# Recurrence keys of the second block mirrored into free columns, one product per level; meta values multiplied over 128 rows

## Chip, cores and metric

One core of one Trainium2 chip. The metric is device time in microseconds of one launch, the median of several executions; one further execution is profiled.

## What is computed

Two transformer blocks in float32 over 256 tokens, width 1024. The first block has differential attention with 16 meta tokens in front, a gated causal convolution of 31 taps and a feed-forward part. The second has attention over blocks (with 256 tokens, plain causal attention of 16 heads), a gated recurrence of 8 heads (hgrn2), attention to a memory of 256 tokens and a feed-forward part. Its recurrence, per head, with keys `k`, queries `q`, values `v` and log decays `g`:

```python
b = cumsum(gc)                                  # within a chunk
diff = b[t] - b[s]
decay = where(causal, exp(diff), 0)
a[t, s] = einsum('td,sd,tsd->ts', qc, kc, decay)
o = o_inter + a @ vc                            # o_inter: from the state before the chunk
```

The first block's attention is, per head, `(softmax(q1 k1) - lam * softmax(q2 k2)) @ v`, where the first 16 keys are the meta tokens.

## The kernel before

Everything is written out per engine (`@block.tensor`, `scalar`, `vector`, `gpsimd`, `sync`), with semaphores between them; each engine runs its list in that order, and no scheduler changes it. Activations lie with channels on the 128 partitions and tokens along the row.

**Weights.** They stream through a ring in 166 chunks of 128x2048 float32. A large product is made of three fast ones: weights and activations are each split into a high part (rounded to fp32r) and a low one, and high x high, high x low and low x high are added (`split_tile` and `split_by_token`, line 570: 24 matmuls a tile, two tiles a chunk). ScalarE rounds a chunk's high parts in two halves (`high_parts`, L1130) once a buffer of two is free; the low parts (`low_half`, L415, ring minus high part) are made one half on VectorE (`low_v`) and one on POOL (`low_g`). In heads1 POOL makes both. TensorE reads the low parts in the last third of a tile. Small products (scores, transposes, values, recurrence) are plain float32 matmuls, each of which is two records in the profile; the "x" counts of TensorE in the rows are records.

**heads1** (4 passes, two of the eight attention heads each, as four units `u`: head and half of the queries). The lists are `heads1` of each engine. Per unit TensorE makes scores (`scores1`, L697), transposes the combined probabilities (`turn1`, L704 for the 16 meta columns, L706) and multiplies the values (`values1`): L713 with the meta tokens' 16 rows (`v_meta[0:META]`, `a1M[0:META]`), then L715 with one or two blocks of 128 rows. VectorE writes maxima (`maxima1`), probabilities (`combine1`, L1711 and L1712) and, in between, the convolution taps (L1750) and its first two columns (`conv_lead`, L1730 to L1734).

**heads2** (4 passes, two recurrence heads and four attention heads each). The recurrence over 256 tokens is treated as two blocks of 128 and the cross part between them. Within a block the lower triangle is split into seven levels, `LEVELS` = 64, 32, ..., 1: on level m each stretch of 2m tokens gives keys from its first half and queries from its second, both scaled by exponentials of the distance to the middle. Per level x, POOL subtracts (L2431, L2432), ScalarE takes the exponential (`decay`, L1428), VectorE multiplies (`level`: keys into `kl`, L2026; queries into `ql`, L2028) and TensorE multiplies block by block (`level`, L930: 128 key columns, of which the unused half is zero, by 64 query columns, twice). `kl` is cleared once by POOL before the loop (L2414). Bank 7 first takes the diagonal (L940) and levels 0 and 1, bank 3 levels 2 to 5, bank 7 then level 6 and the cross product (L954): `hgrn_scores(h, 0..2)`. VectorE gathers them into `amat` (`gather0..2`: L2050 for the diagonal, L2042 a masked copy per level, with masks from the table, L2063). `hgrn_values` (L960, L962) multiplies with the values `iN`, the output of tiles 2 and 3.

Between them stand the attention's steps: rotation (`rotate`, L894; `rope_sin`, `rope_cos`, L2073 to L2078), scores (L903, L904), maxima (L2083 to L2086), exponentials (L1442, L1443), normalising (`normalise2`, L2090 to L2092, which frees `turn2`), transposes (L911), values (L923, L925). `cumulate` (L2009) scans the log decays of the next pass's heads; the fourth pass has none. ScalarE's list around the change is: copies of tiles 2 and 3, parts of chunk 3, `head_keys` (L1438), exponentials of levels 2 and 3, copies of tiles 4 and 5, parts of chunk 4, exponentials of levels 4 and 5, and so on. VectorE's list between the first rotation and the first transposes is: L2073, level 5, `gather0`, L2077 and L2078, level 6, cross products (L2033, L2034), low parts of chunk 5 (L415), `gather1`, second rotation, `gather2`, levels 7 and 8 (the second head's first two), scan, maxima, normalising. POOL's list is subtractions 0, 1, low 2, 2, 3, low 3, 4, 5, 6, low 4, 7, 8, low 5, 9, 10, low 6, 11, 12, 13, low 7 to 9; each subtraction waits until the exponential two before it is done.

## Time and profile before

| | |
|---|---|
| median of 3 runs | 1184.91 us (1183.97 to 1189.07) |
| profiled execution, its own time | 1187.4 us |
| its span, first to last instruction | 1185.8 us |
| mean granted TensorE clock | 0.985 of full speed |
| TensorE (PE) busy | 1141.6 us, 96% |
| VectorE (DVE) busy | 719.4 us, 61% |
| ScalarE (ACT) busy | 600.0 us, 51% |
| POOL (GpSimd) busy | 649.5 us, 55% |

heads1 lies from about 25 to 249 us of the span, down1 from 482 to 544, heads2 from 585 to 841. Busy time is that of instructions; a TensorE instruction's record is longer than its distance to the next, so the chain of waits, which counts from one to the next, gives its cost. PEld are the weight loads, which run beside the matmuls. Where an instruction is blocked after its start, its duration shows it.

### The profile page before, as it was taken

The page shows a single profiled execution, that of the slowest core. Times are in us where ns is not written, and L with a number is a line of the kernel's source. Part 1 is how long each engine was busy: PE and PEld are TensorE (multiplying, and loading weights), DVE is VectorE, ACT ScalarE, POOL GpSimd, SP SyncE. Part 2 cuts the span into 40 slices and gives each one's busy share as a digit, 9 for nine tenths or more (in the row PEclk, how much of TensorE's full clock was granted, in tenths as well). Part 3 has the DMA queues.
Part 4 walks back from the last instruction along what each step waited for, and adds up shares of the span by engine and source line. Part 5 has one row for each costly group of instructions (what it writes and reads, how often), then busy time and mean ns, then how long its engine had stood idle before and what let it go on. Part 6 is the DMA issues. An engine that isn't in the chain of part 4 may idle for free.

```text
span 1185.8 us, 24894 instructions
## 1 busy us (share of the span) xinstructions
PE 1141.6 (96%) x8962; PEld 1095.6 (92%) x8962; DVE 719.4 (61%) x1364; ACT 600.0 (51%) x1112; POOL 649.5 (55%) x451
## 2 busy tenths in 40 slices
PE   6999999999889999999899999999999999999997
PEld 6999999998779999999899989898999989999996
DVE  5675766688656777525875856757666546444322
ACT  5644444455255656437555455555535455444332
POOL 4666666660355666644763637364375436656542
PEclk9999999999889999998999999999999999999998
DMA  8444444341343454543433423333445425545531
GB/s 324 145 147 141 156 141 161 142 147 72 142 178 114 173 192 169 205 148 137 164 126 109 162 99 122 141 109 139 147 174 172 149 90 195 178 177 198 193 143 36
DMA packets 26209, 179.43 MB, mean 151 GB/s; under 512 B 2848, under 2 KB 4128, under 8 KB 4768
## 3 DMA queue, kind: packets, MB, share of 16 engines
q1 hardware_dynamic: 25856, 178.28, 42.2%
q8 instruction: 43, 0.70, 0.2%
q10 hardware_dynamic: 288, 0.27, 0.1%
q14 instruction: 22, 0.18, 0.0%
HBM read 177.49 MB, written 1.05 MB: 151 GB/s over the span
## 4 chain that ended last, share of the span: by engine, by line
PE 77%; DVE 11%; issue 6%; POOL 2%; ACT 2%; DVEq 0%; DMA 0%; POOLq 0%; ACTq 0%
PE ps L570 51%; PE ps L852 10%; PE ps L930 2%; POOL parts L415 2%; PE ps L636 1%; PE ps L485 1%; DVE ps L2185 1%; DVE act L1823 1%; PE ps L667 1%; PE ps L610 1%; DVE branch L1964 1%; PE ps L923 1%; ACT parts L1130 1%; DVE parts L415 1%; PE ps L533 1%
## 5 line engine op out<-in xcount | busy, mean ns | idle before, releaser
L415 POOL TENSOR_TENSOR parts<-ring,parts 128x1024 fp32r<-128x1024 f32 x208 | 513.5, 2479 | 478.2 <-ACT parts L1130 475.1
L570 PE MATMUL ps<-x_high,parts 128*128 128x256 f32 (+2 forms) x3088 | 417.4, 284 | 4.3 <-DVE glu L1999 2.2
L570 PEld LDWEIGHTS ps<-x_high,parts 128*128 128x128 f32 x3088 | 387.2, 189 | 15.1 <-issue 8.1
L1130 ACT ACTIVATE parts<-ring 128x1024 fp32r<-128x1024 f32 x324 | 323.9, 1049 | 138.5 <-PE ps L852 69.3
L415 DVE TENSOR_TENSOR parts<-ring,parts 128x1024 fp32r<-128x1024 f32 x116 | 151.8, 1309 | 127.3 <-ACT parts L1130 127.3
L570 PE MATMUL ps<-x_low,parts 128*128 128x256 f32 (+2 forms) x1520 | 214.5, 284 | 0.0
L570 PEld LDWEIGHTS ps<-x_low,parts 128*128 128x128 f32 x1520 | 196.3, 189 | 0.0
L1750 DVE SCALAR_TENSOR_TENSOR ps<-glu,table_sb,ps 128x256 f32<-128x256 f32 x232 | 93.3, 479 | 0.6 <-DVE ps L1750 0.2
L852 PE MATMUL ps<-act_high,parts 128*128 128x256 f32 x704 | 87.8, 280 | 0.0
L852 PEld LDWEIGHTS ps<-act_high,parts 128*128 128x128 f32 x704 | 85.1, 188 | 0.0
L570 PE MATMUL ps<-parts,x_high 128*128 128x256 f32 x448 | 62.3, 285 | 0.9 <-DVE work L2098 0.9
L570 PEld LDWEIGHTS ps<-parts,x_high 128*128 128x128 f32 x448 | 56.4, 188 | 3.0 <-issue 3.0
L1109 ACT ACTIVATE work<-ps 128x256 f32<-128x256 f32 (+2 forms) x52 | 19.9, 385 | 74.9 <-PE ps L570 72.1
L852 PE MATMUL ps<-act_low,parts 128*128 128x256 f32 x352 | 46.5, 282 | 0.0
L852 PEld LDWEIGHTS ps<-act_low,parts 128*128 128x128 f32 x352 | 43.8, 189 | 0.0
L1100 ACT ACTIVATE work<-work 128x256 f32<-128x256 f32 x44 | 18.3, 418 | 49.0 <-DVE work L2275 33.0
L1100 ACT ACTIVATE work<-ps,table_sb 128x256 f32<-128x256 f32 x44 | 24.5, 558 | 33.7 <-PE ps L570 29.7
L1964 DVE TENSOR_TENSOR branch<-work 128x256 f32 (+1 forms) x22 | 34.4, 1561 | 3.8 <-DVE work L1959 2.3
L2431 POOL TENSOR_TENSOR sq<-conv 128x128 f32 x56 | 25.4, 454 | 19.7 <-ACT sq L1428 16.1
L1100 ACT ACTIVATE sq<-res 128x256 f32<-128x256 f32 (+2 forms) x48 | 18.2, 412 | 34.3 <-DVE res L1873 27.0
L485 PE MATMUL ps<-conv,ring 128*128 128x258 f32 x128 | 31.6, 410 | 3.6 <-DVE x_high L1836 3.6
L485 PEld LDWEIGHTS ps<-conv,ring 128*128 128x128 f32 x128 | 25.6, 205 | 9.3 <-issue 3.9
(331 smaller groups left out, 1611.0 us busy)
## 6 DMA issues: line engine op xcount, KB each, us to landing
ring<-weights SPq DMA_DIRECT2D x166, 1024.0 KB, 4.8
res<-h_in SPq DMA_DIRECT2D x4, 272.0 KB, 3.7
act<-mem SPq DMA_DIRECT2D x1, 1024.0 KB, 14.9
out<-xT SPq DMA_DIRECT2D x4, 256.0 KB, 2.5
table_sb<-table SPq DMA_DIRECT2D x1, 969.5 KB, 9.0
table_sb<-table ACTq DMA_DIRECT2D x1, 132.5 KB, 3.5
work<-positions ACTq DMA_DIRECT2D x1, 128.0 KB, 4.7
```

The lines of the kernel that those rows point to most:

```text
L415: eng.tensor_tensor(parts[:, LOW - HIGH + p, cols], ring[:, slot, cols], parts[:, p, cols].bitcast(F32), ALU.subtract)\
L485: mm = pe.matmul(ps[:, b, 0:width], ring[:, slot, k * CW + e * P:k * CW + e * P + P], moving(k), start=k == 0, stop=k == KB - 1)
L533: mm = pe.matmul(ps[:, 4, c * wide:(c + 1) * wide], sq[:, k, s:s + P], weight(k), start=k == 0 and c == 0, stop=k == KB - 1, skip_group_ch ...
L570: mm = pe.matmul(out, left(k), right(k), start=step_ == 0 and k == 0, stop=step_ == 2 and k == KB - 1)
L852: mm = pe.matmul(ps[:, DOWN_BANK + t // 2, t % 2 * SEQ:(t % 2 + 1) * SEQ], w[:, kk * D + t * P:kk * D + t * P + P], x[:, kb + kk, 0:SEQ], ...
L930: mm = pe.matmul(ps[:, bank, at + HD * blk:at + HD * blk + HD], kl[:, l, blk * P:blk * P + P], ql[:, l, blk * HD:blk * HD + HD], start=Tru ...
L1100: ins = sc.activation(out, src, fn, **kw)
L1109: sc.activation(out, src, fn, scale=scale).then_inc(tile_read[b], 1)
L1130: sc.activation(parts[:, p, cols], ring[:, slot, cols], ACT.Copy).then_inc(split_high, 1)
L1750: ve.scalar_tensor_tensor(acc, u, w, acc, ALU.mult, ALU.add).then_inc(dve_step, 1)
L1964: ve.tensor_tensor(branch[:, j + (e - 2), 0:SEQ], silu_g[:, 2 * (g % 2) + e - 2, :], acc, ALU.mult)\
L2431: gp.tensor_tensor(d[:, :, 0, :], middle, b[:, :, 0, :], ALU.subtract)
```

## The change

1. Mirrored keys. `kl` has 128 columns a level instead of 256. The first block's keys stay in the first halves of each stretch; the second block's are written backwards, so that they fall on the second halves, which were zero. VectorE writes them with a second product, `ql` as before. TensorE makes one product per level, 128 key columns by 128 query columns (both blocks). The keys of a column's other block come out as scores too, and the masks leave them out.
2. What follows from it. The second block's scores have their rows in mirrored order, so its keys for the diagonal (`head_keys`, now four copies of 128 columns) are mirrored, the diagonal is taken with `both_diagonals` (identity and mirrored identity), and the second block's values are mirrored once per pass: `mirror_values`, one product 128x256 on TensorE after tile 4, through bank 2, which ScalarE copies back to `iN[:, 1]`. The masks and `both_diagonals` are made on VectorE during down1 (`mirrored_constants`). The clearing of `kl` on POOL is gone.
3. Meta values. `v_meta` and `a1M` are cleared once by POOL at the start (ScalarE waits for it in the first pass), and `values1` multiplies all 128 rows, where rows 16 to 127 are zero.

```diff
         ones, ident = col("ones", 0, P), col("ident", 0, P)
+        masks = col("level_masks", 0, len(LEVELS) * P).bitcast(I32).rearrange("p (l c) -> p l c", c=P)
...
         kh = carve(gluf, 0, HEADS, SEQ)
+        both_diagonals = carve(gluf, HEADS * SEQ, 2 * P)
         attf = branch[:, :, :].rearrange("p a b -> p (a b)")[:, 2 * KB * TQ:3 * KB * TQ]
...
         kh_s = carve(actf, 4480, 2, SEQ)
-        kl = carve(resf, 0, len(LEVELS), SEQ)
+        kl = carve(resf, 0, len(LEVELS), P)
         cross_e = carve(resf, 1792, 2, P)
...
         meta_shift, meta_exp, meta_probs, meta_T, meta_done = (sem(n) for n in ("meta_shift", "meta_exp", "meta_probs", "meta_T", "meta_done"))
-        att_gated = sem("att_gated")
+        values_mirrored = sem("values_mirrored")
+        att_gated, meta_cleared = sem("att_gated"), sem("meta_cleared")
         centered, conv_root, conv_scaled, conv_act = (sem(n) for n in ("centered", "conv_root", "conv_scaled", "conv_act"))
...
                 hold(pe, bank_read[7], n.before(bank_read[7]))
-                pe.matmul(ps[:, 7, 0:P], v_meta[0:META, h * P:h * P + P], a1M[0:META, :], start=True, stop=False)
+                pe.matmul(ps[:, 7, 0:P], v_meta[:, h * P:h * P + P], a1M, start=True, stop=False)
                 for j in range(u % 2 + 1):
...
+            def mirror_values(i):
+
+                b = STREAM.bank("heads2", 3)
+                hold(pe, bank_read[2], n.before(bank_read[2]))
+                pe.wait_ge(tile_read[b], STREAM.before("heads2", i, 3) + 1)
+                pe.matmul(ps[:, 2, 0:CW], both_diagonals[:, P:2 * P], iN[:, 1, :], start=True, stop=True)\
+                  .then_inc(values_mirrored, 1)
+
             def scores2(j):
...
             def level(h, l, bank, at):
-                for blk in range(2):
-                    mm = pe.matmul(ps[:, bank, at + HD * blk:at + HD * blk + HD], kl[:, l, blk * P:blk * P + P],
-                                   ql[:, l, blk * HD:blk * HD + HD], start=True, stop=True)
-                return mm
+                return pe.matmul(ps[:, bank, at:at + P], kl[:, l, :], ql[:, l, :], start=True, stop=True)
...
-                for t in range(6):
+                for t in range(5):
                     proj(t)
+                mirror_values(i)
+                proj(5)
                 hgrn_scores(0, 0)
...
                 if start:
+                    sc.wait_ge(meta_cleared, 2)
                     root_of_mean(7, SEQ, D, "eps6", root[:, 0:SEQ], rooted)
...
             def head_keys(i, h):
-                sc.activation(kh_s[:, h, :], kh[:, i * 2 + h, :], ACT.Copy).then_inc(khs_ready, 1)
+                sc.activation(kh_s[:, h, 0:P], kh[:, i * 2 + h, 0:P], ACT.Copy)
+                sc.activation(kh_s[:, h, SEQ - 1:P - 1:-1], kh[:, i * 2 + h, P:SEQ], ACT.Copy).then_inc(khs_ready, 1)
...
                 head_keys(i, 1)
+                sc.wait_ge(values_mirrored, n.next(values_mirrored))
+                sc.activation(iN[:, 1, :], ps[:, 2, 0:CW], ACT.Copy).then_inc(bank_read[2], 1)
                 decay(2)
...
-            down_low("down1")
+            def mirrored_constants():
+
+                ve.tensor_copy(both_diagonals[:, 0:P], ident)
+                ve.tensor_copy(both_diagonals[:, P:2 * P], ident[:, ::-1])
+                at = 0
+                for l, m in enumerate(LEVELS):
+                    blocks = ident
+                    if m > 1:
+                        blocks = conv_f[:, at:at + P // m]
+                        step(ve.tensor_reduce(blocks, ident.rearrange("p (j i) -> p j i", i=m), AX, ALU.add))
+                        at += P // m
+                    ve.tensor_copy(masks.bitcast(F32)[:, l, P // 2:P].rearrange("p (b i) -> p b i", i=m),
+                                   blocks[:, ::-2].rearrange("p (b o) -> p b o", o=1).to_broadcast([P, P // (2 * m), m]))
+
+            down_low("down1", mirrored_constants)
             low_v("forget", 0, 0)
...
-            masks = col("level_masks", 0, len(LEVELS) * P).bitcast(I32).rearrange("p (l c) -> p l c", c=P)
-
             def halves(x, m):
...
                 ve.wait_ge(decay_ready, n.next(decay_ready))
-                e = halves(el[:, x % 2, :], m)
-                ve.tensor_tensor(halves(kl[:, l, :], m)[:, :, 0, :], halves(kh[:, i * 2 + h, :], m)[:, :, 0, :],
-                                 e[:, :, 0, :], ALU.mult)
+                e, keys = halves(el[:, x % 2, :], m), halves(kh[:, i * 2 + h, :], m)
+                b = P // (2 * m)
+                ve.tensor_tensor(halves(kl[:, l, :], m)[:, :, 0, :], keys[:, 0:b, 0, :], e[:, 0:b, 0, :], ALU.mult)
+                ve.tensor_tensor(halves(kl[:, l, :], m)[:, ::-1, 1, ::-1], keys[:, b:, 0, :], e[:, b:, 0, :], ALU.mult)
                 ve.tensor_tensor(ql[:, l, :].rearrange("p (b m) -> p b m", m=m), halves(qh[:, h, :], m)[:, :, 1, :],
...
                 ve.wait_ge(bank_full[7], n.next(bank_full[7]))
-                step(ve.tensor_tensor(amat[:, 0:2, :], ps[:, 7, 0:SEQ].rearrange("p (a b) -> p a b", b=P),
-                                      ident.rearrange("p (o b) -> p o b", o=1).to_broadcast([P, 2, P]), ALU.mult))
+                step(ve.tensor_tensor(diag, ps[:, 7, 0:SEQ], both_diagonals, ALU.mult))
                 place(0, 7, 256, dve_step)
...
+            gp.memset(v_meta, 0.0).then_inc(meta_cleared, 1)
+            gp.memset(a1M, 0.0).then_inc(meta_cleared, 1)
             gp.memset(rinv[:, 0:TQ], 0.0).then_inc(pool_step, 1)
...
                 low_g("heads2", 0, c)
-            gp.wait_ge(cum_ready, 2)
-            gp.memset(kl, 0.0).then_inc(pool_step, 1)
-            gp.wait_ge(pool_step, n.next(pool_step))
             with gp.Fori(0, 4) as i:
```

How the instructions stand, first on TensorE around the copy of tile 5 in heads2 (names: `x_high`, `x_low_55` and `parts` are activations and weight parts, `sq` is `ql`, `res` is `kl`). Before, tiles 4 and 5, the diagonal of head 0 and its levels 0 and 1:

```order
L581 ISA
L570 MATMUL ps<-x_high,parts 128x256 x8
L570 MATMUL ps<-x_low_55,parts 128x256 x8
L570 MATMUL ps<-x_high,parts 128x256 x8
L221 REGISTER_ALU
L570 MATMUL ps<-x_high,parts 128x256 x8
L570 MATMUL ps<-x_low_55,parts 128x256 x8
L570 MATMUL ps<-x_high,parts 128x256 x8
L221 ISA
L937 ISA
L938 ISA
L940 MATMUL ps<-work,act 128x128 x2
L930 MATMUL ps<-sq,res 128x64 x4
```

The same place after the change:

```order
L573 MATMUL ps<-x_high,parts 128x256 x8
L221 ISA
L904 REGISTER_ALU
L905 MATMUL ps<-work,glu 128x256
L573 MATMUL ps<-x_high,parts 128x256 x8
L573 MATMUL ps<-x_low_55,parts 128x256 x8
L573 MATMUL ps<-x_high,parts 128x256 x8
L221 REGISTER_ALU
L945 ISA
L946 ISA
L948 MATMUL ps<-work,act 128x128 x2
L940 MATMUL ps<-sq,res 128x128 x2
```

The mirroring product (L905) stands between tiles 4 and 5, and two wide level products take the place of four narrow ones.

On VectorE, heads2, the end of the first rotation's product, level 6, the cross products and the low parts of chunk 5. Before:

```order
L2078 TENSOR_TENSOR work<-work 128x512
L2024 REGISTER_ALU
L2026 TENSOR_TENSOR res<-glu,sq 128x128
L2028 TENSOR_TENSOR sq<-work,sq 128x128
L2032 REGISTER_ALU
L2033 TENSOR_TENSOR sq<-glu,res 128x128
L2034 TENSOR_TENSOR res<-work,res 128x128
L414 ISA
L415 TENSOR_TENSOR parts<-ring,parts 128x1024
```

After:

```order
L2104 TENSOR_TENSOR work<-work 128x512
L2050 REGISTER_ALU
L2053 TENSOR_TENSOR res<-glu,sq 128x64
L2054 TENSOR_TENSOR res<-glu,sq 128x64
L2055 TENSOR_TENSOR sq<-work,sq 128x128
L2059 REGISTER_ALU
L2060 TENSOR_TENSOR sq<-glu,res 128x128
L2061 TENSOR_TENSOR res<-work,res 128x128
L417 ISA
L418 TENSOR_TENSOR parts<-ring,parts 128x1024
```

One product more per level, in two of 64 columns; the order around it is the same.

On ScalarE, heads2, between the parts of chunk 3 and the exponential of level 2. Before:

```order
L1130 ACTIVATE parts<-ring 128x1024 x2
L1438 ISA
L1438 ACTIVATE act<-glu 128x256
L1438 ISA
L1438 ACTIVATE act<-glu 128x256
L1426 REGISTER_ALU
L221 REGISTER_ALU
L1428 ACTIVATE sq<-sq 128x256
```

After:

```order
L1140 ACTIVATE parts<-ring 128x1024 x2
L1449 ISA
L1449 ACTIVATE act<-glu 128x128
L1450 ISA
L1450 ACTIVATE act<-glu 128x128
L1449 ISA
L1449 ACTIVATE act<-glu 128x128
L1450 ISA
L1450 ACTIVATE act<-glu 128x128
L1501 REGISTER_ALU
L1502 ACTIVATE work<-ps 128x256
L1437 REGISTER_ALU
```

Four half copies for two whole ones, and the copy of the mirrored values with its wait (L1501) ahead of the exponential.

## Rows read from the trace of the kernel before

**Rows 1.** The page, part 1: busy us, share of the span, instructions.

```profile
PE 1141.6 (96%) x8962; PEld 1095.6 (92%) x8962; DVE 719.4 (61%) x1364; ACT 600.0 (51%) x1112; POOL 649.5 (55%) x451
```

**Rows 2.** Stretches of heads2's third pass: start:end, length, PE, PEld, DVE, ACT, POOL busy, clock, DMA.

```profile
661.90:727.30 65.40, 65.40 (x511) 60.62 (x510) 43.43 (x100) 34.97 (x77) 32.88 (x37) 1.00 0.36 128
667.20:683.60 16.40, 16.40 (x131) 15.41 (x130) 14.12 (x37) 6.65 (x15) 8.57 (x10) 1.00 0.52 192
```

**Rows 3.** The chain that ended last, third pass of heads2: start us, us, what.

```profile
662.17 0.44 PE ps L940 x4
...
667.21 2.83 PE ps L570 x24
670.04 1.73 PE ps L930 x16
...
683.59 0.33 PE ps L911 x3
...
702.67 0.48 PE ps L911 x3
...
705.99 0.43 PE ps L960 x2
```

**Rows 4.** VectorE in order of time, third pass: start us, us, what [idle before].

```profile
653.59 2.27 DVE L2026 TENSOR_TENSOR res<-glu,sq 128x128 f32<-128x128 f32 x1 [0.15 <-ACT sq L1428]
...
667.25 0.69 DVE L2073 TENSOR_TENSOR work<-ps,work 128x512 f32<-128x512 f32 x1 [1.72 <-PE ps L894]
667.86 0.42 DVE L2026 TENSOR_TENSOR res<-glu,sq 128x128 f32<-128x128 f32 x1
668.20 0.48 DVE L2028 TENSOR_TENSOR sq<-work,sq 128x128 f32<-128x128 f32 x1
...
672.19 1.21 DVE L415 TENSOR_TENSOR parts<-ring,parts 128x1024 fp32r<-128x1024 f32 x1
...
678.83 1.36 DVE L2009 TENSOR_TENSOR_SCAN conv<-table_sb,conv 128x128 f32 x4
...
682.55 0.35 DVE L2092 TENSOR_SCALAR work<-work,small 128x256 f32<-128x256 f32 x1
...
697.80 1.73 DVE L415 TENSOR_TENSOR parts<-ring,parts 128x1024 fp32r<-128x1024 f32 x1
...
701.91 0.35 DVE L2092 TENSOR_SCALAR work<-work,small 128x256 f32<-128x256 f32 x1
```

**Rows 5.** Groups of VectorE: a product of 64 and one of 128 columns.

```profile
L1680 DVE TENSOR_TENSOR table_sb<-table_sb x1: 214/214/214, 19.6 to 19.6; 128x64 f32<-128x64 f32 x1
...
L2034 DVE TENSOR_TENSOR res<-work,res 128x128 f32<-128x128 f32 x8 | 2.2, 280 | 0.0
```

**Rows 6.** POOL in order of time, third pass of heads2.

```profile
653.21 2.50 POOL L415 TENSOR_TENSOR parts<-ring,parts 128x1024 fp32r<-128x1024 f32 x1 [1.75 <-ACT parts L1130]
...
664.97 0.40 POOL L2431 TENSOR_TENSOR sq<-conv 128x128 f32 x1 [1.91 <-ACT sq L1428]
...
665.75 2.37 POOL L415 TENSOR_TENSOR parts<-ring,parts 128x1024 fp32r<-128x1024 f32 x1
...
672.43 3.23 POOL L415 TENSOR_TENSOR parts<-ring,parts 128x1024 fp32r<-128x1024 f32 x1 [1.52 <-ACT parts L1130]
...
696.09 2.35 POOL L415 TENSOR_TENSOR parts<-ring,parts 128x1024 fp32r<-128x1024 f32 x1 [5.06 <-ACT parts L1130]
```

**Rows 7.** The chain that ended last, third pass of heads1, around two values1 calls.

```profile
183.25 0.41 PE ps L713 x2
183.66 0.42 PE ps L715 x2
...
187.66 0.64 PE ps L715 x4
```

**Rows 8.** TensorE in order of time, third pass of heads1, the third transposes.

```profile
176.20 0.28 PE L704 MATMUL ps<-table_sb,work 128*16 128x128 f32 x1 [0.24 <-DVE work L1712]
```

**Rows 9.** VectorE in order of time, a chunk of down1.

```profile
494.55 1.23 DVE L415 TENSOR_TENSOR parts<-ring,parts 128x1024 fp32r<-128x1024 f32 x1 [4.45 <-ACT parts L1130]
```

More of the change, by code:

```diff
@@ L164 @@
 BODY[('tensor', 'heads1')] = {'kv_ready': 1, 'bank_read4': 4, 'probs_ready': 4, 'bank_read6': 4, 'bank_read7': 4}
-BODY[('tensor', 'heads2')] = {'roped': 2, 'bank_read7': 4, 'khs_ready': 2, 'level_ready': 16, 'bank_read2': 3, 'bank_read3': 4, 'bank_read4': 4, 'probs_ready': 4, 'bank_read5': 4, 'bank_read6': 1}
+BODY[('tensor', 'heads2')] = {'roped': 2, 'bank_read7': 4, 'khs_ready': 2, 'level_ready': 16, 'bank_read2': 4, 'bank_read3': 4, 'bank_read4': 4, 'probs_ready': 4, 'bank_read5': 4, 'bank_read6': 1}
 BODY[('scalar', 'heads1')] = {'bank_full4': 4, 'max_ready': 4, 'probs_ready': 4, 'bank_full6': 4, 'bank_full7': 4}
@@ L168 @@
 BODY[('scalar', 'up2')] = {'gate_act': 4}
-BODY[('scalar', 'heads2')] = {'bank_full7': 4, 'diff_ready': 14, 'level_ready': 16, 'bank_full4': 4, 'max_ready': 8, 'bank_full3': 4, 'bank_full5': 4, 'bank_full8': 4}
+BODY[('scalar', 'heads2')] = {'values_mirrored': 1, 'bank_full7': 4, 'diff_ready': 14, 'level_ready': 16, 'bank_full4': 4, 'max_ready': 8, 'bank_full3': 4, 'bank_full5': 4, 'bank_full8': 4}
 BODY[('vector', 'heads1')] = {'bank_full4': 4, 'dve_step': 79, 'bank_read4': 4, 'bank_full6': 4, 'conv_ready': 2}
```

## Prediction

> **What bounds the kernel now.** I read the page first, then the busy time by stretches, then the chain of waits, and at last the instructions in order of time on all four engines through one pass of the heads2 loop (the third, 661.9 to 727.3 us; the other passes repeat it 65.4 us apart). TensorE is busy 96% of the span and through the whole of that pass, which moved nothing but its own work [rows 1, 2]. Read alone, that says: shorten TensorE and the time falls. The next view limits this. I cut a pass at the instructions where TensorE takes something from VectorE: **A**, from the end of the first rotation (L894, 667.21) to the first softmax's transposes (L911, 683.59); **B**, from there to the fourth softmax's transposes (702.67); **C**, the rest. In A VectorE is busy 14.1 of 16.4 us, and what is left are waits for its own last instruction [rows 2]. It starts at 667.25, when the rotation is there, and has the probabilities at 682.55 + 0.35 = 682.90; TensorE takes them at 683.59, some 0.5 later than a handing over needs [rows 3, 4]. In B its chain of normalising, four levels, maxima, weight parts and normalising ends at 701.91 + 0.35 = 702.26, and TensorE takes the result at 702.67: some 0.25 to spare [rows 3, 4]. So A and B are almost as long on VectorE as on TensorE. C has TensorE alone.
>
> **The level products.** Each was two products over 64 columns, now one over 128. Eight old products take 1.73 (each stands as two records), 0.216 a product [rows 3]; two 128-column products of the same type take 0.44, 0.22 a product [rows 3]. A level falls from 0.43 to 0.22. Per pass that is 2 levels in C (0.43), 4 + 1 in A (1.08), 2 + 4 in B (1.30) and the last in B (0.22): 3.0, in four passes 12.1. The added mirroring product (128x256, as L960) costs 0.43 in C [rows 3]. C comes out even, and all depends on what A and B do with their 2.6.
>
> **A.** VectorE gets one product more per level. A 64-column product takes 0.214, a 128-column one 0.280 [rows 5], so splitting one costs two times 64 columns and a second start: 0.07 at least. The upper end is a product beside POOL's subtractions, 0.48 against 0.28, some 0.41 to the next start [rows 4]. A holds levels 5 to 8. TensorE would come to the transposes 1.08 earlier, VectorE gets there 0.3 later at best, and 0.5 lay between: with nothing else, TensorE waits 0.9 and A ends as before. But there is a race. VectorE starts half of chunk 5's weight parts (L415) at 672.19, POOL its half at 672.43, and POOL then takes 3.23 instead of 2.45: it waited. Where POOL is first, VectorE waits: the key product at 653.59 took 2.27, ending when POOL's did, and the weight parts at 697.80 ended 1.09 after POOL's [rows 4, 6]. By these rows the loser of the race pays a whole POOL instruction. The Trainium skill ("SBUF — State Buffer", Who interferes with whom) has this as a rule: a VectorE instruction with two SBUF inputs and a GpSimd one that reads SBUF exclude each other, and the first to start keeps the port for its whole length. By that rule, the trace agrees.
>
> Who is first after the change? The margin is 672.43 - 672.19 = 0.24 [rows 4, 6], and 0.23 to 0.25 in all four passes. The mirroring product stands before tile 5, so tile 5 ends 0.43 later. ScalarE's parts of chunk 4 and the exponential behind them follow it, POOL's subtraction at 664.97 waits for that exponential, and POOL's L415 at 665.75 comes behind it [rows 6]: it now ends at 668.55, not 668.12. The level-5 key product at 667.86 already had to wait for that end [rows 4], so it is 0.43 later, and the added products of levels 5 and 6 give 0.14 more: VectorE comes to its L415 at 672.75 or later. POOL's start hangs on ScalarE's parts of chunk 5, hence on tile 7, which isn't later: the 0.43 before tile 5 is given back by the two levels behind it. POOL is first. VectorE's parts end at 672.43 + 2.45 + 1.09 = 675.97, not 673.40: +2.57, and what follows them is dense. Less 0.1 for POOL work that no longer meets the rotation's products, plus 0.14 for levels 7 and 8: the probabilities come 2.6 later, at 685.5, and TensorE takes them at 685.6 instead of 683.59. **A: +2.0.** I take 0.07 for each added product here, since the row nearest to them, 128 columns in 0.280, ran beside nothing; at 0.41 each, A would end at +2.7, and with VectorE first in the race near 0.
>
> **B.** The second softmax's scores and their maxima move by 2.1. Then come levels 9 to 12 with an added product each, 4 x 0.07 = 0.3 to 4 x 0.41 = 1.6; in the third pass POOL's small subtractions meet only two or three of those products, so 0.4. The weight parts behind them stay second to POOL's, as they are now [rows 6]. The 0.3 that lay before the last transposes hides part: 2.1 + 0.4 - 0.25. **A and B together: +2.25 a pass**, and TensorE's 2.6 goes into three waits. The fourth pass has no scan of the next heads (four instructions, 1.36 [rows 4]) before the first maxima: there the scores and not VectorE come last, +0.9 after A, +1.05 after B. heads2: 3 x 2.25 + 1.05 = **+7.8**.
>
> **The meta values.** values1 multiplies 16 rows before products of 128 rows. In the chain L713 takes 0.41 and the first L715 behind it 0.42, while the next L715, again 128 rows after 128 rows, adds 0.64 - 0.42 = 0.22 [rows 7]. So each change of rows costs 0.19 to 0.20, and a call has two: 0.39. With 128 rows both go. There are 16 calls. In passes 2 to 4 of heads1 the first two stand before the third transposes, where TensorE already waits for VectorE [rows 8]: those six calls give nothing. Ten give 0.39: **-3.9**. The Trainium skill ("TensorE: Matmul & The Clock Gate", Why this matters for your kernels) says that a lone product over 32 rows takes the same time as over 128. By it this part is worth 0; the rows say 0.39 a call, since they also hold the hand-over between sizes. I take the rows. Behind heads1 the convolution's VectorE chain starts from TensorE's meta scores, so the gain goes on to the end.
>
> **At nothing:** the constants on VectorE in down1 (about 15 small instructions, some 4 us) lie in an idle time of 4.45 per chunk [rows 9], and the parts behind them are wanted only when the next chunk's low products begin; without that cover they would cost their 4 us once. The two memsets on POOL come before its first work. The removed memset lies beside tiles. On ScalarE two more key copies and the mirrored copy (0.35 each at most) delay the decays of levels 2 and 3 by 1.0, and VectorE can't use those before POOL's parts end anyway; if it could, POOL's work of 664.97 would still be what is late.
>
> **Sum.** -3.9 + 7.8 + 0 = +3.9. The profiled execution (span 1185.8, time 1187.4) would show about 1191.3; the median of the runs, 1184.9, becomes **1188.8**. About 0.5%, 5.9 us, is what a measurement of this kernel can tell from no change.
>
> **Rivals.**
> 1. *VectorE stays first in the race.* For it: every added product may hide in waits that I count as dense. Against: 0.14 + 0.43 is twice the margin. A then ends +0.2, B +0.1 more, heads2 +1.2: **1182.2**. 0.17.
> 2. *TensorE's own time decides*, as the 96% suggest. For it: no wait for VectorE of over 0.2 is seen in heads2. Against: the ends at 682.90 and 702.26. Full price -12.1 + 1.7 - 6.2: **1168.3**; with room in A alone (4 x 1.08) 1177, in B alone (4 x 1.52) 1175. 0.20.
> 3. *The slower side: each added product waits out a POOL subtraction*, 0.41 instead of 0.07 to 0.1. It decides once POOL's subtractions stand beside levels 9 to 12 in each pass: 4 x 0.34 x 4 = 5.4 more, **1194.2**. 0.08.
> 4. *The widened meta product gains nothing*, by the small-row equality worked into this kernel: +3.9, **1192.7**. 0.05. (That is the TensorE page's rule.)
> The forecast has 0.50, of which 0.12 lies above 1190.8. That the products don't get shorter is no rival of its own: TensorE has time to spare in A and B, and C would lose 1.7.
>
> **Range and chances.** 1176 to 1195 holds the forecast, rivals 1, 3 and 4 and the upper third of rival 2; somewhat under 2 in 10 is left out, nearly all below. Faster by over 0.5%: 0.20 (rival 2). Slower by over 0.5%: 0.12 + 0.08 + 0.05 = 0.25. Within: 0.55.
>
> **What will show it.** Level products half as many and 0.22 each. In each heads2 pass VectorE's weight parts before the copies of levels 2 to 5 last some 3 us instead of 1.2, POOL's 2.45 instead of 3.23, and TensorE waits 1 to 2 us before the first scores (L903 now) and again before the transposes (L911 now). A pass of 67.6 instead of 65.4. Heads1 3.9 shorter, L713's successor at 0.22. I am wrong if POOL's parts still take 3.2, if the passes fall under 65, or if heads1 is as long as before.

## The result, and the profile after

| | before | after |
|---|---|---|
| median of the runs | 1185.57 us (11 runs, 1183.97 to 1189.07) | 1191.41 us (11 runs, ten of them 1190.13 to 1193.77) |
| ratio after to before | | 1.0049, 95% interval 1.0036 to 1.0061 |
| span of the profiled execution | 1185.8 us | 1188.9 us |
| mean granted TensorE clock | 0.985 | 0.989 |

One run of the changed kernel took 3531.9 us and has no part in the ratio. The change costs 5.8 us; the interval leaves out 1, and the cost lies just under the 5.9 us that the prediction took as the least that can be told from no change. Page of the changed kernel, part 1; it answers to [rows 1]:

```profile
PE 1123.9 (95%) x8858; PEld 1079.8 (91%) x8858; DVE 743.8 (63%) x1435; ACT 601.2 (51%) x1124; POOL 645.9 (54%) x452
```

TensorE is busy 17.7 us less and the kernel is slower: what it saved became waiting. The place is found by laying the starts of ScalarE's 324 weight parts (L1130 before, L1140 after) side by side. The difference is -1.3 us at the end of heads1's first pass, -3.6 at the end of heads1, -6.3 from 360 us to 530, -6.8 as heads2 begins, then +2.9 a pass in three passes and +1.5 in the fourth, and +3.2 from there to the end. So heads1 gave 3.6, heads2 cost 10.2, and nothing behind heads2 moved.

The step from -3.6 to -6.8 is not the change. Stretches of the kernel before (start:end, length, busy time of PE, PEld, DVE, ACT, POOL, then clock and DMA):

```profile
250.00:270.00 20.00, 19.71 (x153) 18.70 (x153) 16.77 (x46) 11.63 (x24) 14.21 (x6) 0.91 0.48 171
...
345.00:480.00 135.00, 131.00 (x1058) 129.73 (x1058) 99.92 (x143) 82.85 (x127) 81.23 (x62) 0.97 0.49 170
545.00:585.00 40.00, 35.70 (x275) 35.05 (x274) 29.80 (x53) 26.88 (x48) 22.39 (x15) 0.91 0.41 148
```

The same stretches of the changed kernel:

```profile
250.00:270.00 20.00, 18.80 (x152) 17.86 (x150) 18.04 (x48) 12.33 (x31) 11.21 (x5) 1.00 0.45 159
...
345.00:480.00 135.00, 133.95 (x1094) 132.91 (x1095) 102.77 (x145) 84.03 (x127) 81.59 (x63) 0.99 0.48 168
545.00:585.00 40.00, 36.70 (x296) 35.65 (x296) 33.99 (x55) 25.80 (x42) 26.74 (x22) 0.99 0.40 142
```

The profiled execution of before had more time at TensorE's lower level of 1.2 GHz (0.91 against 1.00 in the first stretch). This is not the change: e4, e6 and e9 below make the changed kernel's instructions there and their profiles show 0.91 in the first stretch, while e5, e7, e8 and e13 show 1.00. So it is luck of one execution, and it is why the spans differ by 3.1 us and the medians by 5.8: the profiled execution of before lies 1.8 over its median, that of the changed kernel 0.9 under its own. The instructions' own sum, 10.2 - 3.6 = 6.6, fits the medians.

Heads1, the chain that ended last, first pass (start us, us, what), after the change:

```profile
51.94 0.22 PE ps L716 x2
52.16 0.22 PE ps L718 x2
...
59.16 0.22 PE ps L716 x2
59.38 0.45 PE ps L718 x4
```

L716 was L713: 0.41 has become 0.22, and its successor's first product is 0.22, where it was 0.42 [rows 7].

Heads2's third pass. VectorE in order of time (start us, us, what, idle before), from the rotation on, with the first L2053 to L2055 for level 5, the second for level 6, and L2060, L2061 for the cross part:

```profile
663.26 0.69 DVE L2099 TENSOR_TENSOR work<-ps,work 128x512 f32<-128x512 f32 x1 [1.21 <-PE ps L897]
663.87 0.88 DVE L2053 TENSOR_TENSOR res<-glu,sq 128x64 f32<-128x64 f32 x1
664.67 0.44 DVE L2054 TENSOR_TENSOR res<-glu,sq 128x64 f32<-128x64 f32 x1
...
668.23 0.21 DVE L2053 TENSOR_TENSOR res<-glu,sq 128x64 f32<-128x64 f32 x1
668.37 0.21 DVE L2054 TENSOR_TENSOR res<-glu,sq 128x64 f32<-128x64 f32 x1
668.50 0.28 DVE L2055 TENSOR_TENSOR sq<-work,sq 128x128 f32<-128x128 f32 x1
668.70 2.48 DVE L2060 TENSOR_TENSOR sq<-glu,res 128x128 f32<-128x128 f32 x1
671.10 0.48 DVE L2061 TENSOR_TENSOR res<-work,res 128x128 f32<-128x128 f32 x1
671.51 1.43 DVE L418 TENSOR_TENSOR parts<-ring,parts 128x1024 fp32r<-128x1024 f32 x1
...
682.06 0.35 DVE L2118 TENSOR_SCALAR work<-work,small 128x256 f32<-128x256 f32 x1
```

POOL beside it, low parts of chunks 4 and 5:

```profile
662.27 2.39 POOL L418 TENSOR_TENSOR parts<-ring,parts 128x1024 fp32r<-128x1024 f32 x1
...
668.53 2.51 POOL L418 TENSOR_TENSOR parts<-ring,parts 128x1024 fp32r<-128x1024 f32 x1 [0.77 <-ACT parts L1140]
```

And every wait of TensorE in that pass:

```profile
671.64 0.49 PE L940 MATMUL ps<-sq,res 128*128 128x128 f32 x2 [1.01 <-DVE res L2061]
676.90 0.48 PE L914 MATMUL ps<-work 64*128 64x128 f32 x2 [1.71 <-DVE work L2104]
682.46 0.55 PE L922 MATMUL ps<-table_sb,work 128*128 128x128 f32 x3 [0.96 <-DVE work L2118]
701.51 0.55 PE L922 MATMUL ps<-table_sb,work 128*128 128x128 f32 x3 [1.25 <-DVE work L2118]
```

The port (that for which VectorE and POOL exclude each other) went to POOL, as forecast, but one step earlier: it is the cross product L2060 that lasts 2.48 instead of 0.28, and the low parts L418 come after it with 1.43. TensorE, which waited for nothing here before, now waits 4.9 us a pass, 3.7 of them in A. By the prediction's cuts (chain of waits) A grew from 16.38 to 682.46 - 663.23 = 19.23, B went from 19.08 to 19.05, and C stayed at 29.9 to 30.0. All of the +2.86 a pass is A.

### The profile page after: what moved, and what is told of

It reads as the page before. It is cut to its first block, busy times and chain, and to the rows that moved or that the text cites. A ratio compares the mean times of both kernels' runs of the same rounds, so it can differ in the third digit from the quotient of the medians.

```text
span 1188.9 us, 24789 instructions
## 1 busy us (share of the span) xinstructions
PE 1123.9 (95%) x8858; PEld 1079.8 (91%) x8858; DVE 743.8 (63%) x1435; ACT 601.2 (51%) x1124; POOL 645.9 (54%) x452
## 3 DMA queue, kind: packets, MB, share of 16 engines
HBM read 177.49 MB, written 1.05 MB: 150 GB/s over the span
## 4 chain that ended last, share of the span: by engine, by line
PE 62%; DVE 18%; issue 9%; POOL 5%; ACT 4%; DVEq 1%; DMA 0%; ACTq 0%; POOLq 0%
PE ps L573 43%; PE ps L855 10%; POOL parts L418 3%; DVE parts L418 2%; PE ps L639 1%; ACT parts L1140 1%; DVE ps L2211 1%; DVE act L1837 1%; PE ps L488 1%; DVE act L2069 1%; DVE branch L1978 1%; DVE sq L2060 1%; POOL sq L2341 1%; PE ps L613 1%; POOL res L2436 1%
## 5 line engine op out<-in xcount | busy, mean ns | idle before, releaser
L418 POOL TENSOR_TENSOR parts<-ring,parts 128x1024 fp32r<-128x1024 f32 x208 | 512.8, 2476 | 480.8 <-ACT parts L1140 477.9
L1140 ACT ACTIVATE parts<-ring 128x1024 fp32r<-128x1024 f32 x324 | 323.9, 1049 | 138.5 <-PE ps L855 69.3
L418 DVE TENSOR_TENSOR parts<-ring,parts 128x1024 fp32r<-128x1024 f32 x116 | 156.2, 1347 | 120.8 <-ACT parts L1140 120.7
```

Of the source, the lines that this page charges most:

```text
L418: eng.tensor_tensor(parts[:, LOW - HIGH + p, cols], ring[:, slot, cols], parts[:, p, cols].bitcast(F32), ALU.subtract)\
L1140: sc.activation(parts[:, p, cols], ring[:, slot, cols], ACT.Copy).then_inc(split_high, 1)
```

## The experiments

For all kernels I measured each pass by records of TensorE: **A** from the start of the first rotation to the start of the first transposes, **B** from there to the fourth transposes, **C** to the next pass's first rotation. For the kernel before:

```profile
666.19 1.02 PE L894 MATMUL ps<-work,table_sb 128*128 128x512 f32 x2
...
683.42 0.49 PE L911 MATMUL ps<-table_sb,work 128*128 128x128 f32 x3
...
702.60 0.55 PE L911 MATMUL ps<-table_sb,work 128*128 128x128 f32 x3
```

A is 17.23 (it holds the rotation, and so is longer than the prediction's), B 19.18. By records A grows by 3.03 with the change and B falls by 0.13, where the chain of waits has +2.85 and -0.03: where TensorE doesn't wait, the record of the first transposes starts 0.17 before its place in the chain (683.42 for 683.59) and that of the fourth 0.07. The pass is the same by both. Passes shown are ones with the clock at 1.00. Others have a stretch at 1.2 GHz and are longer: e5 67.3 and 67.2, e6 67.3, e7 68.6 twice, e13 69.7 and 68.2. Each ratio is to the kernel before on the same chip.

| kernel | ratio (95%) | median us | A | B | C | pass |
|---|---|---|---|---|---|---|
| before | 1 | 1184.4 to 1185.8 | 17.23 | 19.18 | 28.95 | 65.36 |
| changed | 1.0049 (1.0036 to 1.0061) | 1191.4 | 20.26 | 19.05 | 28.92 | 68.23 |
| e1 meta part alone | 0.9965 (0.9952 to 0.9979) | 1181.7 | 17.23 | 19.18 | 28.95 | 65.36 |
| e2 keys alone | 1.0104 (1.0086 to 1.0122) | 1197.6 | 20.24 | 19.07 | 28.92 | 68.23 |
| e5 exponential before both halves | 1.0021 (1.0009 to 1.0034) | 1188.1 | 18.92 | 19.07 | 28.93 | 66.91 |
| e8 exponential between halves | 0.9990 (0.9975 to 1.0004) | 1184.2 | 17.87 | 19.06 | 28.93 | 65.86 |
| e6 low parts of chunk 7 first | 1.0017 (1.0003 to 1.0031) | 1187.1 | 20.26 | 17.73 | 28.93 | 66.92 |
| e7 scan late | 1.0052 (1.0034 to 1.0069) | 1191.8 | 19.15 | 19.02 | 28.93 | 67.10 |
| e9 = e8 + e6 + e7 | **0.9904** (0.9885 to 0.9924) | **1174.6** | 16.76 | 17.69 | 28.93 | 63.38 |
| e10 old keys, e6 + e7, meta | 0.9962 (0.9949 to 0.9975) | 1180.9 | 17.23 | 19.18 | 28.95 | 65.36 |
| e4 mirroring product later | 1.0053 (1.0037 to 1.0068) | 1191.4 | 20.09 | 19.06 | 28.95 | 68.10 |
| e11 split keys on the kernel before | 1.0021 (1.0005 to 1.0038) | 1188.6 | 17.38 | 19.24 | 28.95 | 65.57 |
| e12 the product alone on before | 1.0020 (1.0007 to 1.0034) | 1187.9 | 17.23 | 19.18 | 29.37 | 65.77 |
| e13 levels 0 and 1 made twice | 1.0060 (1.0047 to 1.0073) | 1192.5 | 19.38 | 19.07 | 29.37 | 67.81 |

**The two parts apart.** e1 is the kernel before with

```diff
-pe.matmul(ps[:, 7, 0:P], v_meta[0:META, h * P:h * P + P], a1M[0:META, :], start=True, stop=False)
+pe.matmul(ps[:, 7, 0:P], v_meta[:, h * P:h * P + P], a1M, start=True, stop=False)
```

and the clearing; e2 is the changed kernel without these lines.

> The kernel before with only the meta change (all 128 rows of v_meta and a1M, cleared at the start). If the two parts of the change are independent, heads1 is 3.6 us shorter, as in the profile of the change, and nothing else moves: 1182.0 us against 1185.6. If the gain needed the rest of the change, or came from something else, less than 1 us. If every one of the 16 calls gave its 0.39, 6.2 us: 1179.4.

> The change without its meta part (16 rows again). If the loss lies in the heads2 passes alone (68.25 us a pass for 65.39 in three, 1.5 more in the fourth), it is 10.1 us slower than before: 1195.7, and heads1 as long as before. If the constants made in down1 or the clearing at the start cost something of their own, more than 1198.

e1: 4.1 us faster, heads1 3.6 shorter in its trace, heads2 as before to 0.01. e2: 11.8 by the medians, 12.3 by the ratio; its passes are those of the changed kernel, heads1 is as long as before. Its total is 2 us above the expectation; in its profile heads2 costs 10.1, as expected, so the rest is between executions. By the ratios the two parts come to +0.7% and the whole change to +0.5%, which the intervals allow. By the passes the parts are independent, and the whole loss is in the mirrored keys.

**Is it the port, and nothing else, in A?** e5 holds POOL's parts of chunk 5 back, e8 does it without making VectorE wait:

```diff
 e5
-                ahead2(3)
                 decay(7)
+                ahead2(3)
 e8
-                ahead2(3)
-                decay(7)
+                ahead2(3, lambda: decay(7))
...
                 for half in (1, 0):
                     sc.activation(parts[:, p, cols], ring[:, slot, cols], ACT.Copy).then_inc(split_high, 1)
+                    if half and between:
+                        between()
```

> The changed kernel with ScalarE's exponential of level 7 ahead of its parts of chunk 5. POOL's low parts of chunk 5 then wait until about 7 us after the end of the first rotation instead of 5.3, and VectorE's cross products and low parts (5.5 and 5.9 us after it) come first. Race theory: the cross product takes 0.28 instead of 2.48, VectorE's low parts 1.25, and POOL's run beside the masked copies and the rotation's product from PSUM, which they do not block. VectorE's chain to the first probabilities is 2.5 us shorter; TensorE waits 0.4 there, a pass is 65.9 to 66.2 us, the total about 1183. Rival, that the added products and their collisions are the cost and the race is only where they show: pass over 67.4, total over 1188.

> The changed kernel with ScalarE's exponential of level 7 between the two halves of its parts of chunk 5. In the run with the exponential ahead of both halves VectorE won the port but stood idle 1.03 us for its half. Now VectorE's half is ready when it comes to it, about 5.9 us after the end of the first rotation, and POOL's is ready at about 6.0: VectorE is first by 0.1. If it is, cross products 0.28 each, low parts 1.25 with no idle time before, A 1.0 shorter than in that run (about 17.9 from the start of the first rotation to the transposes, for 20.26 in the changed kernel) and a pass of 65.9; total about 1183.5. If POOL is first by a little, the low parts take 3.5 and the pass 68.

e8's VectorE and then POOL, third pass (L2061, L2062 are the cross products):

```profile
669.74 0.28 DVE L2061 TENSOR_TENSOR sq<-glu,res 128x128 f32<-128x128 f32 x1
669.94 0.28 DVE L2062 TENSOR_TENSOR res<-work,res 128x128 f32<-128x128 f32 x1
670.14 1.21 DVE L418 TENSOR_TENSOR parts<-ring,parts 128x1024 fp32r<-128x1024 f32 x1
...
671.29 2.40 POOL L418 TENSOR_TENSOR parts<-ring,parts 128x1024 fp32r<-128x1024 f32 x1 [2.50 <-ACT parts L1140]
```

Cross product 0.28, low parts 1.21, and POOL right behind them, beside work that it doesn't block. A fell by 2.39, to the 17.9 and the pass of 65.9 that were expected, and the total by 7 us to that of the kernel before. In e5 the cross product was free too, but the exponential waited for POOL's subtraction, ScalarE's parts came late, and VectorE stood 1.03 us idle for them: A 18.92 and not 17.9. That is a miss of 1 us a pass (expected: a pass of 65.9 to 66.2), and e8 was made from it. So losing the port costs 2.4 of the 2.9 us a pass. The other 0.5 stays in e8. There VectorE still comes to the cross product 6.49 after the rotation's start, for 5.59 before; that the 0.5 is what is left of this lateness (the added products and the wait at level 5) is argued, and no run takes it away alone.

**Is B's wait the port as well?** 

```diff
-                low_values(i, 0)
                 low_v("heads2", i, 7)
+                low_values(i, 0)
```

> The changed kernel with VectorE's low parts of chunk 7 ahead of the low parts of the first attention values. VectorE idles 1.7 us there until ScalarE has rounded those values, and its half of chunk 7 is ready at the start of that idle time. It then has the port before POOL: 1.23 us instead of 2.52, inside the idle time. The last maxima of the pass start when the scores are there, 2.4 us earlier, TensorE waits nothing before the fourth transposes (1.25 now), and stretch B is TensorE's own: 17.8 us for 19.05. Pass 67.0 instead of 68.2, total about 1186.5. Rival, that in B something else than this chain is late too: B over 18.6, total over 1189.5. A as it is (the port is lost at the cross product as now).

e6's VectorE and then POOL in B:

```profile
695.66 1.23 DVE L418 TENSOR_TENSOR parts<-ring,parts 128x1024 fp32r<-128x1024 f32 x1
697.25 0.42 DVE L2129 TENSOR_TENSOR ya_low<-ps,ya_high 128x256 f32 x1 [0.37 <-ACT ya_high L1466]
...
696.65 2.47 POOL L418 TENSOR_TENSOR parts<-ring,parts 128x1024 fp32r<-128x1024 f32 x1 [5.13 <-ACT parts L1140]
```

2.52 has become 1.23, POOL's 2.38 is 2.47, B is 17.73: TensorE's own time, as expected.

**Is VectorE's chain all there is in A?** e7 moves the scan into idle time of C:

```diff
-                if scan:
-                    ve.wait_ge(log_ready, 2)
-                    cumulate(i + 1)
                 maxima2(0)
...
                 low_values(i, 1)
+                if scan:
+                    ve.wait_ge(log_ready, 2)
+                    cumulate(i + 1)
```

> The changed kernel with the scan of the next heads (four instructions, 1.36 us in all) moved from ahead of the first maxima to behind the second low parts of attention values, where VectorE idles 2.5 us and 5 us before POOL reads it. If VectorE's chain alone sets A in passes 1 to 3, A is 1.28 shorter there and as it was in the fourth: pass 66.95, three times 1.28, total about 1187.5. If the scan is hidden in A (TensorE's scores late as well), under 0.5 a pass, total over 1190.

In the first pass A is 19.15, 1.1 shorter: right. In the second and third it is 20.69, and the total hasn't moved. The same 10 us of A in its three passes:

```profile
609.00:619.00 10.00, 8.29 (x62) 7.36 (x61) 8.13 (x23) 3.41 (x9) 1.26 (x3) 1.00 0.55 211
676.00:686.00 10.00, 8.29 (x52) 7.58 (x51) 8.12 (x23) 3.33 (x8) 1.24 (x3) 0.83 0.56 210
744.00:754.00 10.00, 8.29 (x51) 7.43 (x52) 8.13 (x23) 3.24 (x9) 1.37 (x3) 0.83 0.56 210
```

Equal busy time, but at 0.83 part of the stretch ran at 1.2 GHz, behind the wait of 1.71 for the scores; it costs 1.54 a pass, more than the scan gave. The seven executions show a mean clock of 0.982 to 0.987, those of the kernel before 0.987 in the mean. So the mechanism was right, and in this profile the lower clock took back what it gave; for the other executions only their mean clock says so. e5, e6 and e13 have such a stretch too, e2 and e4, with as much waiting in a pass, have none in heads2.

**Together, and with the old keys.** e9 is the changed kernel with e8's, e6's and e7's edits. e10 is e1 with e6's and e7's (VectorE has the port there already).

> All three together on the changed kernel: exponential of level 7 between the halves, VectorE's low parts of chunk 7 first, the scan late. If the three causes are all that keeps TensorE waiting in heads2, its own time is left: A 16.2 us (17.23 before, 20.26 in the changed kernel, from the start of the first rotation), B 17.9, C 28.9, a pass of 63.0 for 65.4 before, some 2 us less in the fourth, and with the meta part 13 us under the kernel before: 1173. If a next wait comes up (ScalarE's exponentials or the second rotation), passes of 64 to 65 and 1176 to 1179.

> The kernel before with the meta part, VectorE's low parts of chunk 7 first and the scan late, but with the old keys and the two narrow products a level. There TensorE never waits in heads2, so room on VectorE buys nothing: A 17.23, B 19.18, C 28.95, a pass of 65.4 as before, and the same time as the meta part alone, 0.9965 of the kernel before. Against it the run with all three and the mirrored keys (0.9904) shows what the mirrored keys are worth once VectorE has room: 2 us a pass. If these moves were good by themselves, this run would be under 0.994.

e9 is the fastest kernel of the case: 1174.6 us, 1.0% under the kernel before. Its heads2 has one wait of TensorE left from the first rotation to the fourth transposes:

```profile
672.95 0.48 PE L914 MATMUL ps<-work 64*128 64x128 f32 x2 [0.58 <-DVE work L2105]
```

It is 1.6 us over the expectation: A is 16.76, not 16.2, since VectorE still reaches the scores 0.58 late. e10 has the passes of the kernel before and the time of e1. So the two moves are worth nothing where TensorE sets the pass, and the mirrored keys, a loss of 10 us as they were put in (1.0049 against e1's 0.9965), gain 6 to 7 once VectorE has room (0.9904 against 0.9962). e10 leaves out e8's edit, so that this holds for the old keys with the two moves that they can use.

**What made VectorE late?** e4 moves the mirroring product:

```diff
-                mirror_values(i)
                 proj(5)
                 hgrn_scores(0, 0)
+                mirror_values(i)
```

and ScalarE's copy of it behind `ahead2(2)`. e11 is the kernel before with the key product split in two (`for part in (slice(0, b), slice(b, 2 * b))`, each 64 columns). e12 is the kernel before with a product after tile 4, by the identity, and its copy.

> The changed kernel with the mirroring product after tile 5 and the scores (not after tile 4), and ScalarE's copy of it after the parts of chunk 4. The 0.43 us still lie before the rotation, but no longer between tile 5 and POOL's low parts of chunk 4. Race theory: POOL's low parts of chunk 4 end 0.43 earlier against the rotation, so the keys of level 5 are not blocked (0.44 or less instead of 0.88), VectorE is at the cross product before POOL starts its low parts of chunk 5 and gets the two cross products through (0.2 to 0.5 each), but loses the port for its own low parts of chunk 5, which take 3.3 to 3.7. Pass 67.8 us, total about 1189.5. Rival, that the 0.43 before the rotation and the added products set the pass and the port only shows it: pass unchanged at 68.2.

> The kernel before with VectorE's key product of each level split in two of 64 columns, and nothing else changed: one part of the change alone, with TensorE's work as before. If the added products are enough to lose the port (0.34 at level 5, beside POOL's subtractions, and 0.07 at level 6, against a margin of 0.24), VectorE's low parts of chunk 5 or a cross product take 2.4 to 3.6 us, POOL's low parts there 2.4 to 2.5 instead of 3.23, A is 2.3 to 2.6 longer, a pass 67.7 to 68.1 and the total about 1194. If it takes the mirroring product's 0.43 as well, POOL's parts still take 3.1 or more, A is 0 to 0.3 longer and the total within 2 us of the kernel before.

> The kernel before with the product after tile 4 and ScalarE's copy alone (with the identity, so that the values stay as they are). TensorE has 0.43 more work a pass, VectorE none. If the prediction's step holds, that this product puts POOL's low parts of chunk 4 and with them the level-5 keys 0.43 later and so flips the race alone, A is 2.1 to 2.5 longer and a pass 67.9. If POOL's parts of chunk 4 are held by something that is not later (ScalarE's exponentials before them), VectorE stays first and a pass is 65.8 us: total 1.7 over the kernel before.

All three missed. e4 brought 0.13 a pass, close to its rival's pass of 68.2: the copy now stands before the exponentials that POOL's list waits for, so POOL's parts of chunk 4 were hardly earlier, and VectorE came to the cross product at 6.33 (from the rotation's start), POOL to its parts of chunk 5 at 6.26. e12 flipped nothing and cost its 0.41 in C: the product puts tile 5, the rotation and VectorE later alike. In the changed kernel the rotation comes earlier again against tile 5, by the two narrowed levels between them; that half was missing. e11 made VectorE 0.45 later at the cross product (0.36 for the added product at level 5, beside POOL's subtractions, not 0.07; the rest at level 6), and yet kept the port: POOL's parts 3.70, A +0.15. So neither part alone turned the race. e13 joins them: in the changed kernel levels 0 and 1 of the first head are made twice, so that the rotation stands as late against tile 5 as before.

```diff
+                    if h == 0:
+                        level(h, 0, 7, 256)
+                        level(h, 1, 7, 384)
                     level(h, 0, 7, 256)
                     level(h, 1, 7, 384).then_inc(bank_full[7], 1)
```

> The changed kernel with the first head's products of levels 0 and 1 made twice, between tile 5 and the tile before the first rotation: 0.43 us of pure waste on TensorE a pass, in the place of the 0.43 that the change took out there. If it is the earlier rotation against tile 5 (and so against POOL's low parts of chunk 4) that adds the last 0.46 of VectorE's lateness, the rotation is 0.43 later against POOL, the keys of level 5 are blocked 0.5 and not 0.88, VectorE comes to the cross product about 6.0 after the start of the rotation, as in the run with the split keys alone, and keeps the port: cross products 0.3, low parts 1.25, POOL's 3.7. A about 17.4 for 20.26, B 19.0, C 28.9 + 0.43, a pass of 65.8 for 68.2 and a total some 8 us under the changed kernel, about 1183. If the port is lost all the same, the passes are 68.2 to 68.7 and the total 1191 to 1193.

e13's VectorE and then POOL; the first row is level 5's keys, 0.42 as before the change:

```profile
666.08 0.42 DVE L2056 TENSOR_TENSOR res<-glu,sq 128x64 f32<-128x64 f32 x1
...
670.65 0.28 DVE L2064 TENSOR_TENSOR res<-work,res 128x128 f32<-128x128 f32 x1
670.85 3.41 DVE L418 TENSOR_TENSOR parts<-ring,parts 128x1024 fp32r<-128x1024 f32 x1
...
664.04 2.37 POOL L418 TENSOR_TENSOR parts<-ring,parts 128x1024 fp32r<-128x1024 f32 x1
...
670.66 2.53 POOL L418 TENSOR_TENSOR parts<-ring,parts 128x1024 fp32r<-128x1024 f32 x1 [1.15 <-ACT parts L1143]
```

e11's, which should be the same race:

```profile
672.75 0.32 DVE L2036 TENSOR_TENSOR res<-work,res 128x128 f32<-128x128 f32 x1
672.96 1.25 DVE L415 TENSOR_TENSOR parts<-ring,parts 128x1024 fp32r<-128x1024 f32 x1
...
672.76 3.70 POOL L415 TENSOR_TENSOR parts<-ring,parts 128x1024 fp32r<-128x1024 f32 x1 [1.15 <-ACT parts L1130]
```

The lateness is now accounted for: from the rotation's start VectorE reaches the cross product at 5.59 before, 6.04 with the added products (e11, e13 alike), and 6.50 with level 5's keys blocked 0.46 longer as well. The outcome of the race at 6.04 isn't: POOL starts at 6.24 and VectorE's low parts at 6.44 in both, in each of four passes, and e11's VectorE got the port, e13's POOL (low parts 3.41). So the lateness alone doesn't settle who is first, and why the port was lost in the changed kernel is shown only as far as its lateness goes. One thing differs between the two: e11's products just before last 0.30 to 0.32, e13's 0.28. So e13's expected gain of 8 us did not come; A fell by 0.9 in its first pass (the second and third hold a stretch at the lower clock, and the total is no better), by the blocked time at level 5 and the cross products that slipped through.

## Why the prediction was right or wrong

Predicted 1188.8 with 1176 to 1195, and 0.55 for less than 0.5% either way; measured 1191.4, 5.8 us over the kernel before. That it came out within 0.5% is luck: the forecast was a cost of 3.9, and against the 1184.9 that the prediction started from, 1191.4 is 6.5 more; only against the 1185.57 of 11 runs is it 5.8, just under the line of 5.9. By its steps:

- **What bounds the kernel, and the races: right.** TensorE had 96% and lost 18 us of work for nothing; the end was set by the hand-overs that the prediction cut the pass at. e6, e8 and e9 show that the pass falls as VectorE's chain is freed: in e9 by 1.98 of the 2.6 that TensorE saved, with one wait of 0.58 left. One reading was off: the longest idle time of VectorE in A is a wait of 0.98 for ScalarE's exponentials (before 682.15), not one for its own last instruction. The sum doesn't use it.
- **The level products and C: right.** Two of them take 0.45, C is even (28.92 for 28.95), and the mirroring product costs 0.41 (e12).
- **A, forecast +2.0, measured +2.85: the mechanism right, a term too small.** The text let POOL start at 672.43 - 667.21 = 5.2 after the rotation's end (measured 5.30), take 2.45 (2.51), and put VectorE's low parts 1.09 behind it. It counted lateness of 0.57, with 0.07 for each added product, so VectorE would have its cross products done and be at the low parts when it lost. Its own numbers didn't bear that out: with 0.57 the second cross product comes at 671.98 + 0.57 = 672.55, behind POOL's 672.43, and would have been blocked by the prediction's rule. The lateness was 0.91, since the product at level 5 stands beside POOL's subtractions (0.36, near the 0.41 that the text kept for the range). In fact both cross products were still to come: L2060 ended 0.14 behind POOL, L2061 took 0.41 to the next start, and the low parts took 1.43. They ended 671.51 + 1.43 - 663.23 = 9.71 after the rotation's end, where the text had 675.97 - 667.21 = 8.76: the missing 0.9. So the sign "weight parts of some 3 us instead of 1.2" was not seen; the 2.48 stood one step before them. VectorE's chain to the probabilities grew by 682.41 - 663.23 - 15.69 = 3.49, and 0.64 of it was hidden in the distance to TensorE, which fell from 0.69 to 0.05 (the sum hid 0.6, though the text speaks of 0.5). Of TensorE's waits one was not named: 1.01 for the cross product.
- **The cause of the lateness: argued rightly, priced too low.** The shift of POOL's parts of chunk 4 against the rotation was forecast at 0.43 and is 0.46 at level 5. It needs both the product before tile 5 and the two short levels behind it (e12, e13). What was priced too low are the added products, 0.36 for 0.07 at level 5. That the lateness decides the race is not shown (e11 and e13).
- **B, forecast +0.15, measured 0.** (The text puts A at +2.0 and reckons with 2.1 in B; with 2.0, A and B together come to 2.15 and not 2.25.) Its four added products (0.14 each) filled places where VectorE had stood idle: 0.48 for TensorE's scores, 0.25, and a part of 2.54 for ScalarE before. That TensorE's 1.3 went into one wait at the fourth transposes is as forecast; e6 shows that it too hung on one race, over chunk 7.
- **The fourth pass, forecast +1.05, measured +1.5:** in A +1.8 for 0.9, the same missing 0.9; in B -0.25 for +0.15. heads2 came to 10.2 for 7.8.
- **The meta values, forecast -3.9, measured -3.6 by the trace and -4.1 by e1: right**, down to its structure: four calls gave 1.33 in the first pass and two each gave 0.75 in the others, 0.36 a call. The Trainium skill ("TensorE: Matmul & The Clock Gate", Why this matters for your kernels) puts a lone product over 32 rows at the time of one over 128. No run here has such a product alone: what they show is a product over 16 rows between products over 128, at 0.41 with a successor of 0.42, and 0.22 each when all have 128.
- **At nothing: right.** The constants took 5.1 us on VectorE, with one copy blocked for 2.42, and delayed one low part by 0.6; ScalarE's starts in down1 keep their distance of -6.30 throughout.
- **The rivals.** That VectorE stays first didn't happen; e8 is that case, with 65.86 a pass (the rival's +0.3 is 65.7). That TensorE's own time decides had 0.20: e9, with three edits more, comes near it. The waits of 0.41 for each added product were seen at level 5 only.

## What to carry to other kernels

Where two engines exclude each other at a port, a term of the sum is who comes first, and an edit that makes a third engine faster can move it: list for each such meeting the margin, and what is queued behind the loser. Room on the bounding engine and room on the one that hands over to it must be made together: the keys alone cost 10 us or more, two of the three moves without them gave nothing, and all together gained 6 to 7. Let the long instruction of the other engine fall beside work that reads PSUM (in e8 POOL's low parts stand beside four masked copies, which take 1.78 as before), and give an engine's idle time the part whose input is ready.

## What the hardware showed that I had not expected

- **The race is no simple order of starts.** POOL was first where its record starts 0.07 (e4) or 0.17 (changed kernel) before VectorE's next instruction, and second at 0.25 after it (before). At 0.20 before it, with these starts equal to 0.01 us, e11's VectorE and e13's POOL got the port. The executions of e11 spread from 1184.3 to 1192.7 us, those of the kernel before beside them from 1183.3 to 1189.1; that would fit a race that falls anew in each, but e12, whose passes are all alike, spreads from 1185.1 to 1192.6 as well, and only one execution of each was profiled: it stays open. The Trainium skill ("SBUF — State Buffer", Who interferes with whom) says that whoever issues first gets the shared pair of ports for the whole instruction. The rows here agree that the other waits for the whole of it (2.48, 3.41, 3.70); e11 and e13 show that who is first can't be read from the starts of the records.
- **Equal waits, unequal clock.** In e7 TensorE, busy 8.29 of 10 us in all three passes, kept 2.4 GHz in one and was granted 0.83 in two, 1.54 us each. The changed kernel, e2 and e4, whose waits in a pass are longer in sum, show 1.00 in all passes of their profiles. What decides it is not settled; in e7's profile it took back nearly all that moving the scan had gained.
